# Stage edges: one barrier instead of two, and semaphores cleared by ranges beside the next stage

## What is computed

```python
x = even_layer(x, c, ctx, c_ctx, ...)   # mLSTM and differential attention, then a SwiGLU FFN (2816)
x = odd_layer(x, c, ...)                # gated depthwise convolution, then a top-2 of 8 mixture of experts
for l in range(2):
    x = hybrid_layer(x, c_2, ...)       # three kinds of attention (dsa, fox, nsa), gate, projection, layer norm
```

## Time and profile before

| | |
|---|---|
| median of 3 runs | 2051.98 us (2044.40 to 2054.52) |
| profiled execution, first to last instruction (span) | 2045.0 us |
| instructions | 43367 |
| TensorE busy / weight load | 91% / 74% of the span |
| VectorE, ScalarE, GpSimd busy | 40%, 19%, 0% |
| mean granted TensorE clock | 0.939 |
| HBM read | 476 MB, 233 GB/s over the span |

### The profile page before, as it was taken

One profiled execution on the slowest core, in us unless ns is written; L12 is line 12 of the kernel. 1 busy time (PEld: TensorE's weight loads), 2 busy tenths in 40 slices (PEclk: granted clock), 3 DMA queues, 4 the chain that ended last, 5 costly groups with the idle time before them and its releaser, 6 DMA issues. The chain is left out here.

```text
span 2045.0 us, 43367 instructions
## 1 busy us (share of the span) xinstructions
PE 1857.1 (91%) x18202; PEld 1520.8 (74%) x18202; DVE 826.8 (40%) x2249; ACT 393.4 (19%) x1107; POOL 2.3 (0%) x6
## 2 busy tenths in 40 slices
PE   6999897999979778999998999899969998799987
PEld 4576665888868666798688997798658876688765
DVE  3756552778958712011110101011123755236651
ACT  2232332000014231000000000000022233122331
POOL 0000000000000000000000000000000000000000
PEclk7999997999979888999999999999979988899988
DMA  9522241899964024999999898999973411234100
GB/s 389 229 107 90 117 165 67 327 358 366 367 243 145 21 83 176 420 412 334 387 420 387 303 385 341 420 419 335 390 320 124 185 63 62 83 124 167 40 1 21
DMA packets 67912, 480.24 MB, mean 235 GB/s; under 512 B 7424, under 2 KB 9728, under 8 KB 9856
## 3 DMA queue, kind: packets, MB, share of 16 engines
q1 hardware_dynamic: 67712, 477.39, 59.7%
HBM read 476.31 MB, written 1.05 MB: 233 GB/s over the span
## 5 line engine op out<-in xcount | busy, mean ns | idle before, releaser
L467 PE MATMUL PS<-sb_U,sb_ring 128*128 128x256 f32 (+1 forms) x1456 | 379.7, 419 | 19.6 <-PEq L218 13.1
L467 PEld LDWEIGHTS PS<-sb_U,sb_ring 128*128 128x128 f32 x1456 | 286.2, 200 | 101.0 <-issue 62.8
L1659 PE MATMUL PS<-sb_arena,sb_ring 128*64 128x98 f32 x5632 | 246.3, 247 | 15.8 <-issue 12.9
L1659 PEld LDWEIGHTS PS<-sb_arena,sb_ring 128*64 128x64 f32 x5632 | 240.2, 136 | 22.6 <-issue 19.6
L1687 PE MATMUL PS<-sb_ring,sb_arena 128*64 128x256 f32 x1408 | 161.4, 382 | 5.4 <-issue 4.8
L467 PE MATMUL PS<-sb_arena 128*64 128x128 f32 (+9 forms) x884 | 156.6, 354 | 7.3 <-DVE sb_arena L700 4.4
L738 PE MATMUL PS<-sb_U,sb_ring 128*128 128x256 f32 x704 | 155.4, 383 | 6.1 <-PEq L218 6.1
L738 PEld LDWEIGHTS PS<-sb_U,sb_ring 128*128 128x128 f32 x704 | 134.3, 192 | 27.1 <-issue 8.8
L467 PEld LDWEIGHTS PS<-sb_arena 64*128 64x128 f32 (+4 forms) x884 | 110.7, 178 | 47.2 <-issue 27.0
L1687 PEld LDWEIGHTS PS<-sb_ring,sb_arena 128*64 128x64 f32 x1408 | 100.1, 137 | 54.3 <-issue 7.5
L323 DVE SCALAR_TENSOR_TENSOR sb_arena<-sb_ring,sb_cs,sb_arena 128x256 f32<-128x256 f32 x280 | 135.8, 485 | 10.0
(11 more groups left out here) (343 smaller groups left out, 1616.6 us busy)
## 6 DMA issues: line engine op xcount, KB each, us to landing
sb_ring<-stream SPq DMA_DIRECT2D x450, 1024.0 KB, 8.2
sb_consts<-consts SPq DMA_DIRECT2D x1, 1768.5 KB, 26.5
sb_U<-ctxT SPq DMA_DIRECT2D x1, 1024.0 KB, 7.8
sb_XT<-xT SPq DMA_DIRECT2D x1, 1024.0 KB, 9.6
out<-sb_XT SPq DMA_DIRECT2D x8, 128.0 KB, 2.0
sb_small<-small SPq DMA_DIRECT2D x1, 292.0 KB, 2.7
sb_consts<-consts SPq DMA_DIRECT2D x1, 129.0 KB, 2.8
sb_all_small<-layer_small SPq DMA_DIRECT2D x1, 110.0 KB, 26.5
```

Of the source, the lines that this page charges most:

```text
L467: ins = pe.transpose(o, l, r) if t.turn else pe.matmul(o, l, r, start=s, stop=e)
L1659: ins = pe.matmul(PS[c:c + 64, m % 4, h * T:h * T + n], w[:, h, kt, c:c + 64], src[:, kt, 0:n], start=(kt == 0), stop=(kt == KT - 1))
```

## The change

`Stage.__exit__` closes the block (and so keeps the barrier of L215) and only notes the stage as left over. The next `Stage.__enter__` takes its own new semaphores, then lets GpSimd clear those of the stage left over, and opens its block. Clears go by ranges of consecutive numbers, one instruction for a range. The second barrier is gone, and so is the one at the very end of the program. The two `layer2` stages get names of their own, since the semaphores of both are held at once. `late_inputs` is now cleared at the end too.

```diff
     def clear(self):
-        for s in self.landed:
-            self.nc.gpsimd.sem_clear(s)
-        self.nc.all_engine_barrier()
+        clear_together(self.nc, self.landed)
...
     def __enter__(self):
         self.stack = ExitStack()
         self.sems = {n: self.stack.enter_context(self.nc.semaphore(f"{self.name}_{n}")) for n in self.names}
+        Stage.clear_left(self.nc)
         self.inner = ExitStack()
         self.block = self.inner.enter_context(self.nc.Block())
         return self.block, [self.sems[n] for n in self.names]
 
     def __exit__(self, *a):
         self.inner.close()
-        for s in self.sems.values():
-            self.nc.gpsimd.sem_clear(s)
-        self.nc.all_engine_barrier()
-        self.stack.close()
+        Stage.left.append(self)
+
+    @staticmethod
+    def clear_left(nc):
+
+        while Stage.left:
+            stage = Stage.left.pop()
+            clear_together(nc, list(stage.sems.values()))
+            stage.stack.close()
+
+
+def clear_together(nc, sems):
+
+    numbers = sorted(s.num for s in sems)
+    while numbers:
+        n = 1
+        while n < len(numbers) and numbers[n] == numbers[0] + n:
+            n += 1
+        nc.gpsimd.sem_clear(range(numbers[0], numbers[0] + n))
+        numbers = numbers[n:]
...
-            project("layer2", L2_CH, tasks, stores=...)
+            project(f"layer2_{ly}", L2_CH, tasks, stores=...)
 
+        Stage.clear_left(nc)
         ws.clear()
+        clear_together(nc, [late])
```

More of the change, by code:

```diff
@@ L195, in clear @@
     def clear(self):
-        for s in self.landed:
-            self.nc.gpsimd.sem_clear(s)
-        self.nc.all_engine_barrier()
+        clear_together(self.nc, self.landed)
 class Stage:
+    left = []
     def __init__(self, nc, name, sems):
@@ L2591, in build @@
                     affine(add, "dve", UX[:, k, :], rs[:, k, :], uw[:, k:k + 1], ub[:, k:k + 1], rows_made[k // 4])
-            project("layer2", L2_CH, tasks, stores=[(a["out"][:, k, :], XT[:, k, :], made_x[k]) for k in range(KT)] if final else ())
+            project(f"layer2_{ly}", L2_CH, tasks, stores=[(a["out"][:, k, :], XT[:, k, :], made_x[k]) for k in range(KT)] if final else ())
+        Stage.clear_left(nc)
         ws.clear()
+        clear_together(nc, [late])
 def cols(v):
```

## The result

The changed kernel takes 2025.39 us (median of 6 runs, 2017.58 to 2031.90) against 2048.19 us of the kernel before (6 runs, 2043.70 to 2054.52): a ratio of 0.9904, 95% interval 0.9877 to 0.9930.

A forecast was written before the change was run, and what follows sets the result against it. TensorE, busy 91% of the 2045.0 us span, bounds the stages, while clears and barriers stand on every engine's path at edges. Inner edges 11.8 plus end 2.3 gave 14.1 us: 2052.0 to 2037.9 us, range 2031 to 2046.

The forecast's parts named there:

- What the change removes: Eight inner edges: time from first to second barrier release goes, 11.8 us; at the program's end 2.6 us is on the path.
- What it adds: Range clears on GpSimd: no path cost at inner edges; about four at the end cost 0.3 us, so it gives 2.3.
- one instruction, one price: End of the program: a range clear costs as much as a single clear, 0.071 us, so the end gives 2.3 us.
- the worse bound: Inner edges: a range clearing its semaphores one by one would take 1.85 us, still ending before the barrier or fill behind.
- What moves: After each edge everything starts earlier; DMAs in flight cost zero, at most that edge's 0.4 to 2.1 us if late.
- The clock at equal work: TensorE's return to full clock after edges: if it stayed put, the inner edges' 11.8 us would give only 6.3.
- the full shift: Inner edges: on average the clock's return moves along with TensorE's start, so the whole 11.8 us is gained.
- Cover lost: Rival at the edges: the removed wait hid the fetching of next-stage code; 8.2 us gain, 2043.8 us, chance 0.15.
- Slower: Rival in the layer2 stages: more low-clock stretches, 6.4 us each; three more give 2057.1 us, chance 0.07.
- More than the shift: Rival at the edges: shorter gaps return full clock sooner; one low stretch less, 6.4 us, gives 2031.5, chance 0.08.
- The rival's rate: More than the shift: a low stretch of 13.6 us costs about 13.6 x 0.47 = 6.4 us of TensorE work.
- carried to the median: Sum step: the 14.1 us gain is taken from the median 2052.0, 7.0 above the profiled span, giving 2037.9 us.

The follow-up runs named there:

- the fivefold one: The kernel before with each semaphore of a stage cleared five times instead of once; ratio 1.0177 (1.0143 to 1.0212).
- the 109: All runs of the unchanged kernel before beside the experiments, on every chip; mean 2041.2 us.
- the first two measurements: The changed kernel, 6 runs each, against the kernel before: ratios 0.9904 and 0.9892.
- the last two: The changed kernel again without edit, 12 runs each, against the kernel before: ratios 0.9938 and 0.9942.
- the one-edge kernel: The kernel before with the change only at the edge between the two layer2 stages; ratio 0.9972 (0.9945 to 0.9998).
- the second measurement: The changed kernel repeated without edit, first repeat, against the kernel before; ratio 0.9892 (0.9858 to 0.9926).
- fills: The changed kernel with unread matmuls keeping TensorE busy in the chains closing stages, three versions: long ratio 1.0131, short 2006.80 us, few 2017.62 us.
- the change again, first time: First repeat of the changed kernel, no edit, against the kernel before; ratio 0.9892 (0.9858 to 0.9926).

## Why the prediction was wrong

The steps by their order in the forecast:

- *What the change removes*, 11.8 us at the inner edges: right, 13.08 - 1.32 = 11.76. The gap grew by 0.071 us for each clear added in the kernels with 12 to 36 more at one edge, and by 43.9 us in the fivefold one, where the same price says 42.9.
- *What it adds*: nothing on the path, right; twelve clears, right; the end 2.3 us, measured 2.28. Wrong was "one instruction, one price": a range of 2 takes 45 ns, of 22 158 ns, of 26 175 ns, some 5 ns for each further member. At the inner edges it cost nothing because other work hid it, as it would have hidden the worse bound: single clears there made no edge longer.
- *What moves*: nothing in flight became late. The waits for the ring are 14.1 us in 12 at L1728 (before: 13.5):

```profile
PEld PS L1728 <- DMA sb_ring<-stream: 17.0, 12, 2.7
PE PS L1728 <- DMA sb_ring<-stream: 14.1, 12, 2.5
```

- The clock at equal work: the forecast took the mean, the full shift, and a 6.3 us lower bound. The slope of 0.93 +- 0.04 bears the mean out, right to within a tenth. At the edge to ffn0 the return to full clock did not stay where it was: it came 3.4 us after TensorE's start, 3.2 before.
- *Cover lost*: did not happen, no stage starts with a new wait. *Slower* did not happen either. *More than the shift* did, in the profiled execution: 15.1 us less inside the stages. By the forecast's own sign (stage lengths that change by more than a few microseconds in sum) it was wrong for this execution. The rival's rate was about right: it took 0.47 us for a us of low stretch, and the three stretches that are gone from the second layer2 gave 10.1 us for 20.4.
- **The step that failed** is the level to which the sum was added: "carried to the median, which lies 7.0 above that span, 2052.0 - 14.1 = 2037.9". An execution takes its span plus 1.8 us, so the profiled one took 2046.8 and nothing lies in between that could make 7.0. The median of three was a high draw: single executions of the kernel before have a mean of 2041.2 and a standard deviation of 6.9 us. Starting from that mean the same sum gives 2027.1, and the changed kernel's mean over 36 runs is 2026.4. So of the 12.5 us by which the forecast missed, 10.8 are the level, 0.7 the gain (14.8 instead of 14.1), and 1.0 is that the six runs happened to lie below the mean of the 36. With 1.8 in the place of 7.0 the sum would still have been too high, 2032.7, since the profiled execution was slower than the mean too. The spread of 10.1 us in three runs was on the page; I used it in a rival and left it out of the level and the range.
- The ratio at first sight, 0.9904 instead of 0.9931, is the same fault seen twice: the six runs of before stand 7 us above the mean of the 109. With 6 executions a side and such a scatter a difference has a standard error of some 3.4 us, so 14 us can read as 11 or as 17 without anything behind it; the 23 that it read is 2.7 of these errors off. Two facts stay open: the difference between the first two measurements and the last two is larger than the scatter should allow (10 +- 2.4 us), and the one-edge kernel gained 6.0 +- 1.6 for 1.44. On the chip of the second measurement it is low clock: 14 us more of it in the runs of before, at 0.42 each, are 5.9 of their 6.3 us. Why those runs got more, whether by the chip or by chance, was not settled.

## What to carry to other kernels

A barrier over all engines with serial work behind it cost its full length here, and it could be read to a tenth of a us from two releases. Leaving the second barrier out gave the whole of it whether the work behind it was shortened or not; shortening the work alone gave 8.5 of 11.8 us, and mattered at the end, where nothing covers it. Before adding such a sum to a level, look at how far single runs of the same kernel lie apart, and forecast from the mean of many or with that spread in the range; and look whether several results lean on the same few runs of the kernel before. If most of the spread goes with the granted clock, the waits that lower it are worth more than the edge itself: here a few idle matmuls in each wait gave 20 us, more than all the barriers, and too many of them lost 37.

## What the runs showed of the hardware

The length of the second layer2 took few values in the 16 profiles without fills, with the same instructions. It goes with how long after its first instruction TensorE's clock came back from the low stretch in which the stage begins. Where that was 3.1 to 4.1 us (seven profiles, the changed kernel's among them) the stage took 250.2 to 251.7 us; where it was 5.3 to 6.1 us (eight, before among them), 260.6 to 261.7; in the one between, 4.9 us (the change again, first time), 258.1. The long ones have low stretches of 6.8 us further on, at 94, 128 and 186 us, the short ones have none there. The first layer2 has steps too: 14.4 to 15.1 us went with 258.3 to 260.3, 16.3 to 16.7 with 265.5 to 266.1, 16.8 to 17.5 with 269.0 to 269.9. So a us in where a stage starts against the clock can be worth ten, and one program falls on either side: the changed kernel's second layer2 took 250.5 or 250.6 us in three of its profiles and 258.1 in the fourth. These places are from the clock record of each trace; the rule was found on these profiles and not tried on others.

A us at the lower clock costs an execution 0.42 us on average over all stages. A single clear took 44 ns, and a range clear 45 ns for 2 semaphores, 129 for 17, 158 for 22 and 175 for 26: about 5 ns for each further one.
